# A decoder layer for prompt and samples: SyncE issues every transfer of the samples' key and value pages

## The chip, the cores and the metric

The kernel runs as one program on one core of a Trainium2 chip. The metric is the device time of one execution in microseconds (us), the median of several runs. All engines of the core take part: TensorE (PE) for matrix products and transposes, VectorE (DVE), ScalarE (ACT), GpSimd (POOL), and SyncE (SP), which computes nothing and only issues transfers. Each engine executes its own list of instructions in order and meets the others through semaphores. A transfer between device memory and the on-chip memory is issued by the instruction list of an engine; the bytes are then moved by the core's 16 DMA engines.

## What is computed

One layer of a hybrid decoder runs for a prompt of 512 tokens and for 8 sample sequences of 4 new tokens each. The part that the change touches is the attention of the samples. Each sample has 2048 past tokens, kept as 16 pages of 128 rows in a pool; a page table says which page of the pool holds which stretch of which sample. From the page rows the third and fourth parts, `k_sel` and `v_sel`, are the keys and values of the "selected blocks" branch:

```python
past = cache_kv[page_table].reshape(bsz, past_len, 4, NSA_KV, HEAD_DIM)
...
ks_t = full[:, :, 2].reshape(bsz, nb, BLK, NSA_KV, HEAD_DIM).transpose(0, 3, 1, 2, 4)
vs_t = full[:, :, 3].reshape(bsz, nb, BLK, NSA_KV, HEAD_DIM).transpose(0, 3, 1, 2, 4)
...
imp = jnp.where(allowed, imp, -FORCE_SCORE)
_, idx = lax.top_k(imp, k_sel)
...
s_s = jnp.einsum('bqgrd,bqgksd->bqgrks', qg, ks_g).reshape(bsz, tq, NSA_KV, NSA_REP, k_sel * BLK)
p_s = masked_softmax(s_s, s_mask)
o_s = jnp.einsum('bqgrn,bqgnd->bqgrd', p_s, vs_g)
s_w = jnp.einsum('bqgrd,bngd->bqgrn', qg, wk.astype(F32))
...
o = g[..., 0:1] * o_c + g[..., 1:2] * o_s + g[..., 2:3] * o_w
```

The kernel loads all 16 pages of every sample and applies the choice of blocks as a mask on the scores. A second branch attends to a window of 512 past tokens (`s_w`), a third to compressed blocks (`o_c`). State-space branch, cross-attention and the MLP stand before and after this stage and are not touched.

## The kernel before

**Stages in order.** Input projection and gate products; state-space branch; the samples' pages `k_cmp`, `v_cmp` are loaded (L664), relaid and compressed beside the prompt's attention (L1217 to L1299 on PE); then the samples' attention; then the memory keys, the branch outputs, cross-attention and the MLP. Everything on PE runs in the order in which it is written.

**The samples' attention** runs twice, for two groups (`gg` = 0 and 1) of four samples each. Its pages come in four batches per group, `kc` = 0 to 3: a batch is 4 pages of each of 4 samples, 16 transfers of 128 KB. The function `sel_pages(eng, gg, kc, known)` (L678 to L695) issues one batch on the engine that it is given:

- first it reads the 16 page numbers of the batch from the on-chip copy of the page table (L644: a register load, an operation on the register and a range check each), before any wait;
- then it waits: for group 1 until the four samples of group 0 are done (`sample_pv`, since both groups use one buffer `kv_pg`), for group 0 until the space is no longer used by the compression (`relaid` for `kc` 0, `cmp_done` for the others);
- then it issues the 16 transfers (L693), each counted on the semaphore `kv_in_kc`.

Before the change SyncE issues batches 0 and 1 and GpSimd batches 2 and 3 of each group, each on its own list. On SyncE other work stands between them: in group 0 the `weights(3)` after batch 0, three weight loads of 1 MB for the gate units 0 to 5, and in both groups, after batch 1, the window: for each of the 4 samples a transfer of keys (L809, semaphore `k_win_b`) and one of values (L810), 256 KB each. In group 1 `weights(1)`, one load of 1 MB, stands just ahead of the window.

**PE** takes the batches in the order `KC_ORDER` = (0, 2, 1, 3, 4), where 4 is the window. For each it waits for all 16 transfers, transposes the keys (L1329, 16 transposes) and, one batch behind, computes the scores (L1342); L1346 closes the group's scores. For `kc` = 4 it waits sample by sample:

```python
if kc == 4:
    pe.wait_ge(sem(f"k_win_{b}"), 16 * (gg + 1))
elif b == 0:
    pe.wait_ge(sem(f"kv_in_{kc}"), 16 * 16 * (gg + 1))
```

Then come a gate unit on PE (L999, while VectorE and ScalarE do the softmax), the transposes of the probabilities (L1368), and the product with the values (L1381), whose end is `sample_pv`. The gate units 2 to 4 (L999) run between the groups, and gate unit 0 (L999) ahead of group 0. The next group, and after the second group everything else, follows on PE in order.

Of the kernel before, what the change touches and what calls it, by code (L numbers as in the profile page):

```python
# [52 lines left out]
NG2 = 2  # L53
# [58 lines left out]
def hybrid_decoder_layer(nc, A, O):  # L112
# [7 lines left out]
    with ctx:  # L120
        sems = {}

        def sem(name):
            if name not in sems:
                sems[name] = ctx.enter_context(nc.semaphore(name))
            return sems[name]
# [12 lines left out]
        def place(cols, at=None):  # L139
            if at is None:  # L140
                at = top[0]
                top[0] += cols
            assert at + cols <= ACOLS and not at < ZS < at + cols, (at, cols)
            return upper[:, at - ZS:at - ZS + cols] if at >= ZS else arena[:, at:at + cols]
# [103 lines left out]
        CU = 4  # L248
# [55 lines left out]
        def keys_page(b, kc):  # L304

            return kv_pg[:, KV_AT[kc % 4], b, :, 0:P]

        qbd = place(256, R + 25920).rearrange("p (b c) -> p b c", b=DB)
# [141 lines left out]
        for m in range(4):  # L450
            for q in range(4):
                add(("down", m * 4 + q), KD, 256,
                    [(whole, cols(A["w_down"][0][q * 1024:(q + 1) * 1024, :], m * 256))])
        index = {name: i for i, (name, _) in enumerate(chunks)}
        arrived, _n = [], [0] * RING
        for i, (_, parts) in enumerate(chunks):
            _n[i % RING] += 16 * len(parts)
            arrived.append(_n[i % RING])
# [28 lines left out]
        late_at = {name: i for i, name in enumerate(late)}  # L487
        unsplit = ("in", "gate", "glu", "xk", "xv", "bs", "bn", "bs+bn")
        split_chunks = [i for i, (name, _) in enumerate(chunks) if name[0] not in unsplit]
        split_at = {chunks[i][0]: n for n, i in enumerate(split_chunks)}  # L490
        DN0 = split_at[("down", 0)]
# [112 lines left out]
        def step(name):  # L604

            return sem(step_of[name][0]), step_of[name][1]

        def signal(ins, name, n=1):
            if name in step_of:
                s, at = step_of[name]  # L610
                assert signalled.get(s, 0) == at - 1, (name, signalled)
                signalled[s] = at
                ins.then_inc(sem(s), 1)
            else:
                ins.then_inc(sem(name), n)
# [26 lines left out]
        def known_pages(eng, seqs, first, last):  # L642

            return {(q, p): eng.value_load(page_ids[0:1, q * PAGES + p:q * PAGES + p + 1], min_val=0, max_val=NPOOL - 1)  # L644
                    for q in seqs for p in range(first, last)}

        def raw_relaid(eng, j):

            for half in range(2):
                eng.wait_ge(sem(f"relaid_{half}"), j + 1)  # L650
# [27 lines left out]
        def sel_pages(eng, gg, kc, known):  # L678

            known.update({(gg * 4 + b, p): page for b in range(4)  # L680
                          for (_, p), page in known_pages(eng, (gg * 4 + b,), kc * 4, kc * 4 + 4).items()})
            if gg:
                eng.wait_ge(sem("sample_pv"), 4 * gg)
            elif kc == 0:
                raw_relaid(eng, 13)
            else:
                eng.wait_ge(sem("cmp_done"), 2 * CU - (kc == 2))
            for b in range(4):
                q = gg * 4 + b
                for i in range(4):  # L690
                    p = kc * 4 + i
                    page = known[q, p] if (q, p) in known else known_pages(eng, (q,), p, p + 1)[q, p]
                    eng.dma_start(kv_pg[:, KV_AT[kc], b, i:i + 1, :],  # L693
                                  A["cache_nsa_kv"][0][bass.ds(page, 1), :, 2:4].rearrange("n p z g d -> p n (z g d)"))\
                        .then_inc(sem(f"kv_in_{kc}"), 16)  # L695
# [5 lines left out]
        def _(sp):  # L701
# [3 lines left out]
            def weights(n=1):  # L705
                for _ in range(n):
                    i = nxt[0]
                    nxt[0] += 1
                    if i >= RING:
                        sp.wait_ge(*freed(i - RING))  # L710
                    for dst, src in chunks[i][1]:
                        sp.dma_start(dst, src).then_inc(w_sem[i % RING], 16)
# [50 lines left out]
            known = known_pages(sp, range(4), 0, SP_PAGES)  # L763
# [31 lines left out]
            win = A["cache_win_kv"][0]  # L795
            for gg in range(NG2):
                sel_pages(sp, gg, 0, known)
                if gg == 0:
                    raw_relaid(sp, 4 * CU - 1)
                    weights(3)  # L800
                sel_pages(sp, gg, 1, known)
                if gg == 0:
                    sp.wait_ge(*step("prompt_attn_done"))
                else:
                    weights(1)
                for b in range(4):
                    w = win[gg * 4 + b].rearrange("(n p) z g d -> z p n (g d)", p=P)
                    sp.wait_ge(sem("s_mm"), gg * 20 + b + 1)
                    sp.dma_start(keys_page(b, 4), w[0]).then_inc(sem(f"k_win_{b}"), 16)  # L809
                    sp.dma_start(v_win[:, b], w[1]).then_inc(sem("v_win_in"), 16)  # L810
# [65 lines left out]
        def _(pool):  # L876
# [39 lines left out]
            known = known_pages(pool, range(4), SP_PAGES, PAGES)  # L916
# [7 lines left out]
            for j in range(4 * CU):  # L924
# [8 lines left out]
                    zero_blocks(1, "w1b_zeroed")  # L933
                if j in (8, 9):
                    known.update(known_pages(pool, (j - 2,), SP_PAGES, PAGES))
            for gg in range(NG2):
                sel_pages(pool, gg, 2, known)
                if gg == 0:
                    pool.wait_ge(sem("cmp2_mm"), CU)
                    signal(pool.memset(qbd, 0.0), "qbd_zeroed")  # L940
                sel_pages(pool, gg, 3, known)

            def inverse_rms(n):

# [2127 lines left out]
```

## Time and profile before

| | us |
|---|---|
| median of 3 runs | 1246.42 (1246.36 to 1249.7) |
| time of the profiled execution | 1245.2 |
| its span | 1243.5 |
| PE busy | 1162.8 (94%) |
| DVE / ACT / POOL busy | 652.7 / 454.0 / 168.9 |

The span is what the trace covers; 1.7 us of the profiled execution's time lie around it. Instants are in us from the span's start. In the rows a number in front is the start, the next one the length. In square brackets stands how long an engine sat idle before a row and what ended that. SPq and POOLq are the instruction lists of SyncE and GpSimd; a transfer's row there is its issue, and its landing is told apart. Clock 1.00 in a row is TensorE at its upper level (2.4 GHz), and 0.50 would be the lower one (1.2 GHz).

### The profile page before, as it was taken

What the parts mean: (1) busy time and instruction counts of PE and PEld (TensorE: products, weight loads), DVE (VectorE), ACT (ScalarE), POOL (GpSimd) and SP (SyncE); (2) the same over time, 40 slices, a digit from 0 to 9 for tenths busy, and PEclk for the clock granted to TensorE, in tenths of its full rate; (3) what the DMA queues carried; (4) which work ended last, traced back from release to release, by engine and by line L of the source; (5) the groups of instructions that cost most, each with busy time, mean ns of one, the idle gap of its engine ahead of it and who ended that gap; (6) DMA issues with size and microseconds to landing.
All of it is one profiled execution on the core that took longest, in us unless ns stands there. A gap on an engine that the chain in (4) does not pass through costs nothing.

```text
span 1243.5 us, 21862 instructions
## 1 busy us (share of the span) xinstructions
PE 1162.8 (94%) x8426; PEld 1033.7 (83%) x8426; DVE 652.7 (52%) x1179; ACT 454.0 (37%) x726; POOL 168.9 (14%) x276
## 2 busy tenths in 40 slices
PE   6999988989989989889999997899999999999997
PEld 5888777667867757678897996789999999999997
DVE  3549857546656450511255556546443325666663
ACT  3100101045567451510133546446342325555551
POOL 0100012472531304100001002002000000001000
PEclk9999967989999999999999999899999998999998
DMA  6661512463563825655464643364353232223201
GB/s 191 145 211 38 175 46 94 128 170 97 148 160 93 268 81 188 220 190 150 138 206 132 225 136 112 121 242 136 102 170 102 71 100 69 72 99 102 69 1 72
DMA packets 166770, 163.88 MB, mean 132 GB/s; under 512 B 41526, under 2 KB 147859, under 8 KB 166459
## 3 DMA queue, kind: packets, MB, share of 16 engines
q1 hardware_dynamic: 157658, 134.84, 35.6%
q0 software_dynamic: 9008, 27.65, 7.0%
q8 instruction: 67, 1.10, 0.4%
q14 instruction: 37, 0.30, 0.1%
HBM read 154.08 MB, written 12.53 MB: 134 GB/s over the span
## 4 chain that ended last, share of the span: by engine, by line
PE 74%; SPq 9%; DVE 7%; issue 4%; ACT 3%; DMA 2%; POOL 0%; DVEq 0%; ACTq 0%
PE banks L1478 22%; PE banks L1733 14%; PE banks L999 14%; PE banks L1432 4%; SPq L664 3%; PE banks L1217 3%; SPq L644 2%; PE banks L1414 2%; PE banks L1005 1%; SPq L693 1%; PE banks L1120 1%; PE banks L1381 1%; DVE rounded L2803 1%; PE banks L1269 1%; PE banks L1329 1%
## 5 line engine op out<-in xcount | busy, mean ns | idle before, releaser
L1478 PE MATMUL banks<-rounded 128*128 128x288 f32 (+1 forms) x2304 | 298.1, 290 | 2.1 <-DVE rounded L2849 1.6
L1478 PEld LDWEIGHTS banks<-rounded 128*128 128x128 f32 x2304 | 292.7, 189 | 5.8 <-issue 2.9
L999 PE MATMUL banks<-arena 128*128 128x256 f32 x960 | 228.4, 399 | 3.2 <-issue 1.8
L999 PEld LDWEIGHTS banks<-arena 128*128 128x128 f32 x960 | 183.7, 193 | 40.4 <-issue 1.9
L1733 PE MATMUL banks<-rounded 128*128 128x272 f32 x1536 | 196.3, 291 | 3.8 <-DVE rounded L3031 3.8
L1733 PEld LDWEIGHTS banks<-rounded 128*128 128x128 f32 x1536 | 195.7, 191 | 4.4 <-issue 3.1
L2803 DVE TENSOR_TENSOR rounded<-arena,rounded 128x2048 fp32r<-128x2048 f32 x54 | 125.5, 2324 | 59.8 <-ACT rounded L1924 59.7
L3031 DVE TENSOR_TENSOR rounded<-arena,rounded 128x1088 fp32r<-128x1088 f32 x64 | 82.9, 1304 | 61.4 <-ACT rounded L2168 61.4
L1924 ACT ACTIVATE rounded<-arena 128x2048 fp32r<-128x2048 f32 x54 | 102.9, 1906 | 5.6 <-DMA arena<-in_w_out 5.6
L2168 ACT ACTIVATE rounded<-arena 128x1088 fp32r<-128x1088 f32 x64 | 71.1, 1114 | 82.2 <-PE banks L1733 81.0
L2964 DVE TENSOR_TENSOR arena<-arena 128x256 f32<-128x256 f32 (+1 forms) x64 | 28.1, 440 | 86.3 <-ACT arena L2009 86.3
L2009 ACT ACTIVATE arena<-banks 128x256 f32<-128x256 f32 (+1 forms) x64 | 25.4, 397 | 126.4 <-PE banks L1478 126.4
L1432 PE MATMUL banks<-arena 128*128 128x256 f32 (+1 forms) x256 | 60.5, 394 | 2.0 <-DVE arena L2795 2.0
L1432 PEld LDWEIGHTS banks<-arena 128*128 128x128 f32 x256 | 48.1, 190 | 12.5 <-DVE arena L2795 3.4
L970 POOL TENSOR_TENSOR upper<-upper 128x544 f32<-128x544 f32 x5 | 8.7, 1737 | 306.5 <-ACT upper L2179 306.3
L664 POOL DMA_DIRECT2D arena<-in_cache_nsa_kv x70 | 39.2, 563 | 65.2 <-issue 36.3
L693 POOL DMA_DIRECT2D upper<-in_cache_nsa_kv x64 | 34.5, 539 | 91.5 <-issue 52.0
L950 POOL TENSOR_SCALAR arena<-arena 128x1 f32<-128x1 f32 (+1 forms) x22 | 9.5, 432 | 258.4 <-ACT arena L1908 213.4
L1793 ACT ACTIVATE arena<-banks 128x256 f32<-128x256 f32 (+1 forms) x30 | 10.3, 393 | 93.6 <-PE banks L999 82.7
L2795 DVE TENSOR_TENSOR arena<-banks,arena 128x256 f32<-128x256 f32 (+1 forms) x32 | 14.1, 440 | 47.2 <-PE banks L1432 47.2
L1864 ACT ACTIVATE arena<-banks,arena 128x512 f32<-128x512 f32 (+3 forms) x64 | 33.1, 525 | 15.7 <-DVE arena L2613 15.6
L1858 ACT ACTIVATE arena<-banks 128x1024 f32<-128x1024 f32 (+3 forms) x32 | 22.5, 704 | 34.8 <-PE banks L1269 34.6
(432 smaller groups left out, 1462.9 us busy)
## 6 DMA issues: line engine op xcount, KB each, us to landing
arena<-in_w_up SPq DMA_DIRECT2D x22, 1024.0 KB, 5.5
arena<-in_w_down SPq DMA_DIRECT2D x16, 1024.0 KB, 5.1
arena<-in_w_in SPq DMA_DIRECT2D x13, 1024.0 KB, 6.9
upper<-in_cache_nsa_kv SPq DMA_DIRECT2D x64, 128.0 KB, 2.6
upper<-in_cache_nsa_kv POOLq DMA_DIRECT2D x64, 128.0 KB, 4.8
arena<-in_w_out SPq DMA_DIRECT2D x8, 1024.0 KB, 6.7
arena<-in_cache_mem_kv SPq DMA_DIRECT2D x16, 512.0 KB, 7.2
arena<-in_cache_nsa_kv SPq DMA_DIRECT2D x90, 64.0 KB, 2.3
```

What stands on the lines that cost most here:

```text
L664: eng.dma_start(rows[:, p:p + 1, :], A["cache_nsa_kv"][0][bass.ds(page, 1), :, v].rearrange("n p g d -> p n (g d)"))\
L693: eng.dma_start(kv_pg[:, KV_AT[kc], b, i:i + 1, :], A["cache_nsa_kv"][0][bass.ds(page, 1), :, 2:4].rearrange("n p z g d -> p n (z g d)"))\
L999: ins = mm(bank(b + h, (NA, NB)[h], rows=M), lhsT(k), rhs[:, k, toks], start=(k == 0), stop=(k == K - 1))
L1217: ins = mm(bank(6, n), w1[part][:, d % 32, :], relaid[part][:, d % 32, 0:n], start=(d == 0), stop=(d == HD - 1))
L1432: ins = mm(bank(b, N), c[:, k0 + k, c0:c0 + P], act[:, k, toks], start=(k == 0), stop=(k == 3))
L1478: ins = mm(bank(b, N), w[:, k], a[:, k, toks], start=(k == 0 and z == 0), stop=(k == K - 1 and z == 2))
L1733: ins = mm(bank(4 * (m % 2) + 2 * j + h, HALF), w[:, k, j * P:(j + 1) * P], h_split[:, t % 3, p, i, h * HALF:(h + 1) * HALF], start=(t % 1 ...
L1864: signal(fn(p_sb[:, i % 2, g, 0:n], bank(2 * (i % 2) + g, n), ACT.Exp, bias=nmx[:, at:at + 1], accum_out=rsum[:, at:at + 1]), "p_ready")
L1924: signal(fn(w_hi[:, n % 2], ring[:, i % RING, :], ACT.Copy), "w_hi")
L2168: signal(fn(h_split[:, t % 3, 0], h_tiles(t), ACT.Copy), "h_hi")
L2803: signal(tt(w_lo[:, n % 2], ring[:, split_chunks[n] % RING, :], w_hi[:, n % 2].bitcast(F32), ALU.subtract), "w_lo")
L3031: signal(tt(h_split[:, t % 3, 1], h_tiles(t), h_split[:, t % 3, 0].bitcast(F32), ALU.subtract), "h_lo")
```

## The change

Batches 2 and 3 of both groups move from GpSimd's list to SyncE's, in the order in which PE takes the batches: 0, 2, 1, 3. GpSimd keeps the `memset` of `qbd` and its wait.

```diff
             for gg in range(NG2):
                 sel_pages(sp, gg, 0, known)
+                sel_pages(sp, gg, 2, known)
                 if gg == 0:
                     raw_relaid(sp, 4 * CU - 1)
                     weights(3)
                 sel_pages(sp, gg, 1, known)
+                sel_pages(sp, gg, 3, known)
                 if gg == 0:
                     sp.wait_ge(*step("prompt_attn_done"))
                 else:
...
-            for gg in range(NG2):
-                sel_pages(pool, gg, 2, known)
-                if gg == 0:
-                    pool.wait_ge(sem("cmp2_mm"), CU)
-                    signal(pool.memset(qbd, 0.0), "qbd_zeroed")
-                sel_pages(pool, gg, 3, known)
+            pool.wait_ge(sem("cmp2_mm"), CU)
+            signal(pool.memset(qbd, 0.0), "qbd_zeroed")
```

The number of transfers and their bytes stay. The page numbers of each moved batch are now read by SyncE, 64 reads more on its list. Line numbers behind the first edit grow by two (L809 becomes L811).

**SyncE, group 0.** L644 are the reads of page numbers (16 in a block), L693 the page transfers (16 in a batch), L712 weights, L809 and L810 the window. Before:

```order
L693 ISA [waits relaid_1,relaid_0]
L693 DMA upper<-in_cache_nsa_kv 128x256
...
L712 DMA arena<-in_w_in 128x8x256 [waits lin_done,relaid_1,relaid_0]
L712 DMA arena<-in_w_in 128x8x256 [waits lin_done] x2
L644 TENSOR_LOAD page_ids
L644 ISA x2
...
L693 ISA [waits cmp_done]
L693 DMA upper<-in_cache_nsa_kv 128x256
...
L809 DMA upper<-in_cache_win_kv 128x4x128 [waits s_mm,vector_steps_done]
L810 DMA arena<-in_cache_win_kv 128x4x128
```

The same stretch of SyncE after the change, where L811 and L812 are the window:

```order
L693 ISA [waits relaid_1,relaid_0]
...
L644 TENSOR_LOAD page_ids
...
L693 ISA [waits cmp_done]
...
L712 DMA arena<-in_w_in 128x8x256 [waits lin_done,relaid_1,relaid_0]
L712 DMA arena<-in_w_in 128x8x256 [waits lin_done] x2
...
L693 ISA [waits cmp_done]
...
L693 ISA [waits cmp_done]
...
L811 DMA upper<-in_cache_win_kv 128x4x128 [waits s_mm,vector_steps_done]
L812 DMA arena<-in_cache_win_kv 128x4x128
```

A block of reads and a batch now stand between batch 0 and the weights, and another block and batch between batch 1 and the window.

**GpSimd, group 0.** Before, batches 2 and 3 stood around the `memset` (L940):

```order
L644 TENSOR_LOAD page_ids
L644 ISA x2
...
L693 ISA [waits cmp_done]
L693 DMA upper<-in_cache_nsa_kv 128x256
...
L940 MEMSET upper 128x256 [waits cmp2_mm]
...
L693 ISA [waits cmp_done]
...
L693 ISA [waits sample_pv]
```

Of this only the `memset` and its wait stay on GpSimd. In group 1 both moved batches go ahead of the weight load and the window on SyncE, as in group 0; the order on PE is unchanged.

## Rows read from the trace of the kernel before

**Rows 1.** The page: busy time of each engine, and the chain by engine.

```profile
PE 1162.8 (94%) x8426; PEld 1033.7 (83%) x8426; DVE 652.7 (52%) x1179; ACT 454.0 (37%) x726; POOL 168.9 (14%) x276
PE 74%; SPq 9%; DVE 7%; issue 4%; ACT 3%; DMA 2%; POOL 0%; DVEq 0%; ACTq 0%
```

**Rows 2.** Timeline of PE, group 0: gate unit 0, transposes, scores, gate unit 1.

```profile
425.51 7.60 PE L999 MATMUL banks<-arena 128*128 128x256 f32 x32
...
437.67 1.95 PE L1329 MATMUL banks<-arena,upper 128*128 128x128 f32 x16
...
443.43 1.97 PE L1329 MATMUL banks<-arena,upper 128*128 128x128 f32 x16
...
449.69 0.66 PE L1329 MATMUL banks<-arena,upper 128*128 128x128 f32 x4 [0.89 <-DMA upper<-in_cache_win_kv]
450.28 3.61 PE L1342 MATMUL banks<-upper 128*32 128x512 f32 x16
...
454.90 7.57 PE L999 MATMUL banks<-arena 128*128 128x256 f32 x32 [0.89 <-issue]
```

**Rows 3.** Timeline of PE, group 1, from the gate units between the groups on.

```profile
473.30 22.17 PE L999 MATMUL banks<-arena 128*128 128x256 f32 x96
...
498.72 1.94 PE L1329 MATMUL banks<-arena,upper 128*128 128x128 f32 x16
...
505.09 3.53 PE L1329 MATMUL banks<-arena,upper 128*128 128x128 f32 x16 [3.44 <-DMA upper<-in_cache_nsa_kv]
...
512.44 2.19 PE L1329 MATMUL banks<-arena,upper 128*128 128x128 f32 x16
514.56 1.93 PE L1342 MATMUL banks<-upper 128*32 128x512 f32 x16
516.30 0.31 PE L1346 MATMUL banks<-arena,upper 128*32 128x32 f32 x16
```

**Rows 4.** Timeline of SyncE's list, both groups (start, length, issues).

```profile
391.01 8.69 SPq L693 DMA_DIRECT2D upper<-in_cache_nsa_kv  x16
399.80 7.25 SPq L712 DMA_DIRECT2D arena<-in_w_in  x3
416.36 9.88 SPq L693 DMA_DIRECT2D upper<-in_cache_nsa_kv  x16
440.67 0.39 SPq L809 DMA_DIRECT2D upper<-in_cache_win_kv  x1
...
472.94 26.71 SPq L693 DMA_DIRECT2D upper<-in_cache_nsa_kv  x32
499.69 0.50 SPq L712 DMA_DIRECT2D arena<-in_w_in  x1
501.67 0.39 SPq L809 DMA_DIRECT2D upper<-in_cache_win_kv  x1
```

**Rows 5.** Timeline of GpSimd, the batches of both groups.

```profile
398.68 9.45 POOL L693 DMA_DIRECT2D upper<-in_cache_nsa_kv  x16 [32.08 <-issue]
416.55 0.32 POOL L940 MEMSET upper<- 128x256 f32 x1 [8.42 <-PE banks L1235]
473.41 9.44 POOL L693 DMA_DIRECT2D upper<-in_cache_nsa_kv  x16 [36.34 <-PE banks L1381]
```

**Rows 6.** Landing of transfers: the weights at 399.8 to 400.9, then batch 0.

```profile
DMA to landing us min/median/max: 11.5/15.1/17.5
DMA to landing us min/median/max: 2.0/2.2/3.3
```

**Rows 7.** Busy time, clock, DMA share and GB/s in stretches of the span.

```profile
400.00:417.00 17.00, 17.00 (x151) 13.15 (x150) 9.36 (x27) 9.63 (x23) 7.71 (x15) 1.00 0.98 324
497.00:517.00 20.00, 16.16 (x138) 11.35 (x136) 9.71 (x19) 11.36 (x23) 3.96 (x8) 0.91 1.07 349
182.00:204.00 22.00, 11.81 (x164) 10.59 (x162) 13.67 (x44) 4.27 (x4) 4.26 (x8) 0.69 0.46 139
```

**Rows 8.** Timeline of PE: 32 products of a gate unit's size early in the span.

```profile
172.75 9.81 PE L999 MATMUL banks<-arena 128*128 128x256 f32 x32
```

## The prediction, made before the changed kernel ran

> **What bounds the kernel now.** I read the page first. PE is busy 94% of the span and carries 74% of the chain that ended last; SyncE's list is the second largest part of that chain, with 9%, and POOL has none of it [rows 1]. So what SyncE does late can already hold PE up, and what GpSimd does is off the path. Then I read the timelines of PE, SyncE and GpSimd side by side over the samples' attention, since the order of PE is fixed and only the arrival of pages can move it.
>
> Before group 0, PE has gate unit 0 at 425.51 and then takes batches 0, 2, 1, 3 one after the other, the fourth at 443.43; it waits 0.89 us for the last window keys, resumes at 449.69, and starts gate unit 1 at 454.90 [rows 2]. In group 1 the gate units 2 to 4 cover 473.30 to 495.47 (start plus length). Then PE waits 3.44 us for the pages of batch 1, resumes at 505.09 and ends the scores at 516.61 (516.30 + 0.31) [rows 3]. The pages are hardly late now, because two lists issue them at once: SyncE needs 8.69 us for a batch of 16 and GpSimd 9.45 us or 9.44 us, over the same time [rows 4, 5].
>
> **The price of a batch on SyncE.** Issuing takes 8.7 us. The row of 32 issues in group 1 lasts 26.71 us [rows 4]. Two batches of 8.69 explain 17.38 of it; the other 9.3 us are the 16 reads of page numbers ahead of the second batch. The gap in group 0 between the end of the weights at 407.05 and batch 1 at 416.36 is 9.3 us too [rows 4]. So one more batch costs 9.3 + 8.7 = 18.0 us of SyncE's time. Four such batches are moved, and none of their reads can run earlier, since the list is in order. What hid them before was GpSimd's own list, and that cover goes.
>
> **Group 0, step by step on SyncE** (the instants of before are kept until something moves).
> - Batch 0 ends at 391.01 + 8.69 = 399.7 [rows 4]. Reads 9.3 and batch 2, 8.7, end at 417.7. GpSimd issued batch 2 from 398.68 on [rows 5], so the wait for `cmp_done` is over long before.
> - The three weight loads follow. They took 7.25 us before, because the third issue had to wait [rows 4], in a stretch where the DMA engines were full (share 0.98, 324 GB/s) [rows 7] and GpSimd's batch was in the same engines. Without a full engine it would be about 1.5 us (three issues of 0.50, as the one at 499.69 [rows 4]). After the change nothing competes, but 3 MB still queue: some 1.2 MB must drain before the third is accepted. This is my estimate from half of 324 GB/s over the 7.25 us; at the full rate the same bytes take about 4 us. I take 5.0 us and 0.1 of gap, ends 1.5 and 7.25. That gives 422.8.
> - Reads 9.3, batch 1 8.7, reads 9.3, batch 3 8.7: 458.8. Batch 1 took 9.88 before [rows 4], with the weights still landing; I keep 1.2 us for the upper end.
> - The window starts there instead of at 440.67. Before, PE resumed on the last window keys at 449.69, 9.0 us later [rows 2, 4]; now 467.8. From there to gate unit 1 it was 454.0 - 449.7 = 4.3 us without the idle 0.89 [rows 2]; the scores end at 472.1 instead of 454.0. **Group 0: +18.1 us**, ends +14.6 and +21.5.
>
> Two waits appear inside this and cost nothing extra. Behind SyncE's batch 2 stand the weights of gate unit 0, which land some 7 to 11.5 us after issue (the lower end my estimate for an empty queue, from 1 MB at 324 GB/s and the 3.3 us landing of a page transfer; the upper end measured [rows 6, 7]), at 425 to 429 against a need at 425.51. A delay of up to 4 us there is covered, since PE will sit waiting for batches 1 and 3 anyway: batch 3 lands near 461 (2.2 us after its issue [rows 6]) against a start at 443.43 before. And GpSimd's `memset` waits only for a PE product and ran at 416.55 [rows 5]; it can only come earlier.
>
> **Group 1**, counted from the end of group 0, which has moved as a whole. SyncE reads batch 0's numbers before the wait, in idle time, as before. From 472.94 it issues batch 0, reads, issues batch 2 until 499.65, exactly the 26.71 us that batches 0 and 1 took [rows 4]. Batches 1 and 3 with their reads add 36.0: 535.7. Then the weight load and the window. In group 0 the window alone took 9.0 us from first issue to PE's resuming. In group 1 it took about 14.3 us from 499.69 to the last transposes (near 514.0, the last quarter of the row at 512.44) [rows 3, 4], of which 1.5 us (500.19 to 501.67) were a wait for PE that is over by then; and then the engines were overfull (share 1.07, 349 GB/s) [rows 7]. One MB more than group 0's window at 324 GB/s is 3.2 us, so 9.0 + 3.2 = 12.2; against 14.3 - 1.5 = 12.8 I take 12.5, ends 9.0 and 14.3. PE resumes at 548.2, and 4.3 us later, as in group 0, the scores end at 552.5, against 516.6: **+35.9 us**. With group 1's own tail of 2.6 us (514.0 to 516.6) it would be 1.7 less; ends +30.7 and +37.7.
>
> **The clock.** PE will idle for some 15 us in group 0 and 30 us in group 1. The granted clock fell to 0.91 in 497 to 517 around an idle of 3.44 us, and to 0.69, a mix of both levels, in 182 to 204, where PE was busy 11.81 of 22 us [rows 7]. Just after such a sparse stretch work runs at the lower level: transposes took 3.53 us for 16, instead of 1.97 [rows 2, 3]. Part of this is in the 4.3 us. A gate unit that was partly caught cost 9.81 us instead of 7.57 [rows 2, 8], 2.2 more. I add 1 us per group, 2.0, ends 0 and 5.
>
> **Nothing gives it back.** After group 1 everything on PE stands behind `sample_pv`, and the memory loads too. What the change removes is GpSimd's work, off the path, and the 3.44 and 0.89 us of waiting are replaced by longer waits. Sum: 18.1 + 35.9 + 2.0 = 56.0 us. The profiled execution took 1245.2, so it would take 1301.2; the median of before lies 1.2 above that execution, so 1302. The ends add to +45 and +64: 1291 to 1311.
>
> **The rule against this.** The rows show that the issue of one 128 KB transfer by SyncE takes 8.69 / 16 = 0.54 us, and with the read of its page number 1.13 us [rows 4], while its bytes at 349 GB/s [rows 7] need 0.38 us: here the list, not the DMA engines, is what limits. The Trainium skill, page "DMA: Bandwidth & Descriptors", section "Issuing engines are not separate DMA queues", says that transfers started by SyncE, ScalarE or GpSimd run on the same 16 engines, and that issuing from several only saves the sequencer's time, "which is usually small relative to the DMA itself". By its first half the change would cost nothing; its "usually" fails on these rows by a factor of three. As a rival it stands below, worked out in rows.
>
> **The rivals.**
> - *Bytes set the pace, no change.* If only the bytes counted, group 1's 8 MB of pages, 1 MB of weights and 2 MB of window at 349 GB/s take 33 us from 472.94 on, to 506, ahead of PE's need at 512.44: about 1246. For it speaks that the engines were full in two stretches [rows 7]; against it that SyncE's 32 issues alone lasted 26.71 us. By the skill's sentence this is the expected case. Chance 0.04.
> - *Faster.* The right order ends the wait for batch 1 (3.44), the clock dip behind it (3.53 - 1.97 = 1.6) and the wait for the window (0.89): -5.9 us, about 1240. This holds only if four batches are issued while gate units 2 to 4 run, 22.17 us, so below 5.5 us a batch; measured is 8.7 without the reads. Chance 0.04.
> - *The reads are hidden*, because registers keep the numbers or the reads overlap the issues. Then the four extra blocks of 9.3 us drop out: 56.0 - 37.2 = 18.8, about 1265. Against it: the reads stand in SyncE's list between the batches, and the existing block shows up in full in the 26.71. Chance 0.05.
> - *Dearer.* Gate unit 0 waits for its weights and the lower clock lasts through the gate units behind each group (two more units at 2.2 us, and 3 to 5 us for slower landings): above 1311. Chance 0.07.
>
> **Chances.** The forecast, 1291 to 1311, has 0.80, and the range is its own. Below it lie the three cheaper cases, 0.13 together. A measurement of this kernel tells a change from none at about 0.3%, 4 us. Faster 0.04, same 0.04, slower 0.92.
>
> **What would show each step right.** On SyncE, three blocks of about 9.3 us between four batches of 8.7 in each group; batch 3 of group 1 issued some 62.7 us after the first (26.71 + 36.0). On PE, long waits for pages ahead of the third and fourth batch, then for the window, at L1329 in both groups; gate unit 1 starting some 18 us later, the last score of group 1 some 54 to 56 us later; all stages from there on as long as before. Wrong would be the forecast if SyncE's blocks shrink, if the weight loads stall much longer than 7 us, or if PE's later stages change length.

## The result: slower by 3.3 to 3.4%

| | us |
|---|---|
| changed kernel, median of 4 runs | 1288.73 (1285.95 to 1293.24) |
| changed kernel once more, median of 5 runs | 1288.71 (1286.71 to 1291.5) |
| kernel before, median of 17 runs beside the second measurement | 1248.75 (1242.15 to 1252.71) |
| ratio, first and second measurement | 1.0342 (1.0313 to 1.037), 1.0333 (1.0304 to 1.0363) |

The brackets hold the fastest and the slowest run, for a ratio its 95% interval. The change costs 40 to 42 us. I had forecast 56 us and 1291 to 1311: the direction and the place are right, the size is not, and the time lies 2.3 us under my range.

The page of the changed kernel, engines and chain, answers to [rows 1]:

```profile
span 1284.3 us, 21862 instructions
...
PE 1161.9 (90%) x8426; PEld 1031.0 (80%) x8426; DVE 651.1 (51%) x1179; ACT 455.0 (35%) x726; POOL 134.3 (10%) x212
...
PE 67%; SPq 15%; DVE 7%; issue 6%; ACT 2%; DMA 2%; POOL 0%; DVEq 0%; ACTq 0%
...
L1327 PE MATMUL banks<-arena,upper 128*128 128x128 f32 x160 | 25.4, 321 | 46.7 <-DMA upper<-in_cache_nsa_kv 45.0
```

PE does the same work (1162.8 us before), SyncE's part of the chain went from 9% to 15%, and one line, the transposes of the page keys (L1327, before L1329: behind the edit of GpSimd's list the line numbers fall by two), has 46.7 us of PE's idle time ahead of it, 45.0 of them ended by page transfers. GpSimd gave up 34.6 us of work that had been on nobody's path.

The timeline of SyncE's list, against [rows 4]. The row of 32 issues is two batches with one block of reads between, the row of 64 four batches with three blocks:

```profile
387.53 26.33 SPq L693 DMA_DIRECT2D upper<-in_cache_nsa_kv  x32
413.97 4.90 SPq L712 DMA_DIRECT2D arena<-in_w_in  x3
427.80 25.85 SPq L693 DMA_DIRECT2D upper<-in_cache_nsa_kv  x32
453.77 0.39 SPq L811 DMA_DIRECT2D upper<-in_cache_win_kv  x1
...
484.09 60.95 SPq L693 DMA_DIRECT2D upper<-in_cache_nsa_kv  x64
545.08 0.43 SPq L712 DMA_DIRECT2D arena<-in_w_in  x1
```

The timeline of PE over both groups, against [rows 2, 3]; the brackets hold the idle time ahead of a row:

```profile
422.04 7.60 PE L997 MATMUL banks<-arena 128*128 128x256 f32 x32
...
438.57 1.97 PE L1327 MATMUL banks<-arena,upper 128*128 128x128 f32 x16 [1.45 <-DMA upper<-in_cache_nsa_kv]
...
455.97 3.67 PE L1327 MATMUL banks<-arena,upper 128*128 128x128 f32 x16 [14.44 <-DMA upper<-in_cache_nsa_kv]
...
463.13 1.92 PE L1340 MATMUL banks<-upper 128*32 128x512 f32 x16
...
466.05 7.57 PE L997 MATMUL banks<-arena 128*128 128x256 f32 x32 [0.88 <-issue]
...
511.91 1.97 PE L1327 MATMUL banks<-arena,upper 128*128 128x128 f32 x16 [1.88 <-DMA upper<-in_cache_nsa_kv]
...
529.32 3.67 PE L1327 MATMUL banks<-arena,upper 128*128 128x128 f32 x16 [14.45 <-DMA upper<-in_cache_nsa_kv]
...
547.62 3.67 PE L1327 MATMUL banks<-arena,upper 128*128 128x128 f32 x16 [12.76 <-DMA upper<-in_cache_nsa_kv]
...
556.72 1.92 PE L1340 MATMUL banks<-upper 128*32 128x512 f32 x16
...
559.65 7.57 PE L997 MATMUL banks<-arena 128*128 128x256 f32 x32 [0.88 <-issue]
```

The long waits are 12.8 to 14.5 us. In group 0 there is one, for batch 3; batch 1 is only 1.45 us late, since it had been early before. In group 1 there are two, for batches 1 and 3; batch 2 is late too, by 1.88 us. Meanwhile the DMA engines have time to spare. These are stretches of the changed kernel (columns as in [rows 7]) in which batches are being issued, the last with PE mostly waiting:

```profile
400.00:417.00 17.00, 16.21 (x150) 12.34 (x146) 10.53 (x32) 10.99 (x25) 0.32 (x1) 1.00 0.49 153
...
490.00:517.00 27.00, 22.22 (x125) 17.79 (x123) 7.53 (x15) 7.73 (x17) 0.00 (x0) 1.00 0.37 113
517.00:545.00 28.00, 5.54 (x24) 3.48 (x24) 0.69 (x1) 2.39 (x4) 0.00 (x0) 0.58 0.47 141
```

A share of 0.37 to 0.49, where the kernel before had 0.98 and 1.07 in its busiest stretches [rows 7].

### The profile page after: what moved, and what is told of

It reads as the page before. It is cut to its first block, busy times and chain, and to the rows that moved or that the text cites. A ratio compares the mean times of both kernels' runs of the same rounds, so it can differ in the third digit from the quotient of the medians.

```text
span 1284.3 us, 21862 instructions
## 1 busy us (share of the span) xinstructions
PE 1161.9 (90%) x8426; PEld 1031.0 (80%) x8426; DVE 651.1 (51%) x1179; ACT 455.0 (35%) x726; POOL 134.3 (10%) x212
## 4 chain that ended last, share of the span: by engine, by line
PE 67%; SPq 15%; DVE 7%; issue 6%; ACT 2%; DMA 2%; POOL 0%; DVEq 0%; ACTq 0%
PE banks L1476 21%; PE banks L1731 14%; PE banks L997 13%; SPq L644 5%; SPq L693 4%; PE banks L1430 4%; SPq L664 3%; PE banks L1412 2%; PE banks L1215 1%; PE banks L1003 1%; PE banks L1379 1%; DVE rounded L2801 1%; DMA upper<-in_cache_win_kv 1%; PE banks L1118 1%; SPq L771 1%
## 5 line engine op out<-in xcount | busy, mean ns | idle before, releaser
L1327 PE MATMUL banks<-arena,upper 128*128 128x128 f32 x160 | 25.4, 321 | 46.7 <-DMA upper<-in_cache_nsa_kv 45.0
L1327 PEld LDWEIGHTS banks<-arena,upper 128*128 128x128 f32 x160 | 22.0, 166 | 54.5 <-DMA upper<-in_cache_nsa_kv 49.5
L1885 ACT ACTIVATE upper<-banks 128x512 f32<-128x512 f32 x40 | 21.8, 604 | 57.2 <-PE banks L1327 57.1
```

The source lines that it names most:

```text
L1327: ins = pe.transpose(bank(KT_BANKS[b], P, i * P), keys_page(b, kc)[:, i, :], ident)
```

## Experiments

A difference in us is the measured ratio times the time of the kernel before; that of the two medians differs from it by up to 2 us. Two theories stood at the start. **A**: SyncE's list sets the pace, by its issues and by its reads of page numbers, which stand in order with them. **B**: the reads lie beside other work, and the issues or the bytes are what costs. A group's cost in a trace comes from three starts on PE, gate unit 0, gate unit 1 and the gate unit behind group 1: in the kernel before 425.51, 454.90 [rows 2] and 517.49, in the changed kernel 422.04, 466.05 and 559.65. They moved by -3.5, +11.1 and +42.2 us, so group 0 costs 11.1 + 3.5 = 14.6 us and group 1 42.2 - 11.1 = 31.0. The row of before that [rows 3] do not have:

```profile
517.49 7.57 PE L999 MATMUL banks<-arena 128*128 128x256 f32 x32 [0.88 <-issue]
```

**The reads taken away.** The three later batches use batch 0's page numbers.

```diff
-            known.update({(gg * 4 + b, p): page for b in range(4)
...
+            if kc == 0:
...
-                    page = known[q, p] if (q, p) in known else known_pages(eng, (q,), p, p + 1)[q, p]
+                    page = known[q, i]
```

> The changed kernel, but the page numbers of batches 2, 1 and 3 are not read: all four batches of a group fetch the pages of batch 0 (so the output is computed from the wrong past rows; the transfers keep their number, size and order). Theory A, SyncE's list is the limit and a read block costs it 8.9 us: six blocks leave the list between batches. Group 0: 387.5 + 2 x 8.7 + 4.9 + 2 x 8.7 = 427, ahead of PE, so no loss. Group 1: four batches end 34.8 us after the group before, the window 11 us later and the scores 2.6 us after that, 48.4 us against 43.7 before: +5 us. In all 1252, within 4 us. Theory B, the reads lie beside other work and the 128 issues are what costs: within 5 us of the changed kernel, 1284 to 1293.

Measured: 1253.37 us, ratio 1.005 (1.0028 to 1.0072), +6 us against the kernel before. Nearly the whole loss is gone, as A wants. (This run also fetches the same pages four times over; a run with the right pages, below, gets most of the loss back too.) The list in this trace:

```profile
390.84 16.24 SPq L693 DMA_DIRECT2D upper<-in_cache_nsa_kv  x32
...
475.15 32.81 SPq L693 DMA_DIRECT2D upper<-in_cache_nsa_kv  x64
```

Four batches take 32.81 us, 8.2 each. With the reads they took 60.95, so a block of 16 reads costs (60.95 - 32.81) / 3 = 9.4 us of the list.

**The reads added, nothing else moved.**

```diff
                 sel_pages(sp, gg, 0, known)
+                known_pages(sp, range(gg * 4, gg * 4 + 4), 8, 12)
...
                 sel_pages(sp, gg, 1, known)
+                known_pages(sp, range(gg * 4, gg * 4 + 4), 12, 16)
```

> The kernel before, where SyncE in addition reads the 16 page numbers of batch 2 behind batch 0, and those of batch 3 behind batch 1, and does nothing with them; GpSimd issues batches 2 and 3 as before. Theory A: group 0 +1 to +3 us (window from 442 on instead of 440.7), group 1: batch 1 issued until 508.4 (499.7 before), window from 517 on, scores end at 531 instead of 516.6, +14 us. In all +16 us, 1264, within 4 us. Theory B: reads cost nothing, within 4 us of the kernel before. A third, that SyncE's reads and GpSimd's get in each other's way: a read takes clearly more than the 0.55 us of before and the loss is above 20 us.

Measured: 1262.25 us, ratio 1.0123 (1.0098 to 1.0148), +15 us. The reads alone, with GpSimd issuing its batches as ever, cost more than a third of the loss. The third theory in the expectation falls too: SyncE's register loads took 0.26 to 0.28 us as before, also from 484.8 to 493.0, where GpSimd read its own numbers. SyncE's 32 issues of group 1 now span two blocks instead of one, 35.53 us instead of 26.71, and the window follows a third block later:

```profile
475.48 35.53 SPq L693 DMA_DIRECT2D upper<-in_cache_nsa_kv  x32
519.87 0.39 SPq L712 DMA_DIRECT2D arena<-in_w_in  x1
```

**One group at a time.** The other group's batches 2 and 3 stay on GpSimd.

```diff
+                if gg == 0:
+                    sel_pages(sp, gg, 2, known)
...
+            sel_pages(pool, 1, 2, known)
+            sel_pages(pool, 1, 3, known)
```

> Only group 0 has batches 2 and 3 on SyncE (order 0, 2, 1, 3); group 1 is issued as before, batches 2 and 3 by GpSimd. To keep GpSimd's and SyncE's counts apart, SyncE's two moved batches count on semaphores that are done with their first use. If the loss is the sum of two stages: group 0's part as in the trace of the changed kernel, +14.7 us, group 1's part zero: 1263, within 4 us. If the groups depend on each other (group 0's delay gives SyncE or the clock something back in group 1): below +9 us or above +20.

> Only group 1 has batches 2 and 3 on SyncE; group 0 is issued as before. Semaphores as in the run with group 0 alone. If the loss is the sum of two stages: +31 to +33 us, 1280, within 4 us, and with the run of group 0 alone it adds up to the change's +41 to +46. If group 1 costs what I forecast for it, 36 to 37 us: 1284 or more.

Measured: group 0 alone 1256.83 us, ratio 1.0071 (1.0044 to 1.0098), +9 us; its trace has +13.0 us in group 0. Group 1 alone 1277.97 us, 1.0255 (1.0224 to 1.0286), +32 us; its trace has +31.0 in group 1. The two add up to +41, as the whole change, so the groups cost what they cost separately. Group 1 costs 31 to 32 us, not the 36 to 37 that I forecast. For group 0 the expectation of 1263, within 4, was missed: +9 us lies on the edge that I had set for groups that depend on each other. What speaks against that is the sum. Why the timed runs show 9 us (5.5 to 12.2 by the interval) where three traces have 13.0 to 14.6 is not shown.

**Half the bytes.** The transfers fetch the keys and leave out the values.

```diff
-                    eng.dma_start(kv_pg[:, KV_AT[kc], b, i:i + 1, :],
-                                  A["cache_nsa_kv"][0][bass.ds(page, 1), :, 2:4]...
+                    eng.dma_start(kv_pg[:, KV_AT[kc], b, i:i + 1, 0:P],
+                                  A["cache_nsa_kv"][0][bass.ds(page, 1), :, 2]...
```

> The changed kernel, but each page transfer fetches the keys only, 64 KB instead of 128 KB (the values are left out, so the output is not the layer's). Issues, reads and order stay. If SyncE's list sets the pace, a batch still takes 8.4 to 8.7 us and the time stays within 4 us of the changed kernel (1285 to 1293); the third weight load may be accepted up to 2 us sooner. If the bytes or the landing set it, the two groups' waits shrink with the bytes: below 1275.

Measured: 1287.91 us, ratio 1.0312 (1.0283 to 1.0341); the changed kernel has 1288.7. Group 1's four batches and the weights in group 0:

```profile
417.66 2.71 SPq L712 DMA_DIRECT2D arena<-in_w_in  x3
...
487.09 60.98 SPq L693 DMA_DIRECT2D upper<-in_cache_nsa_kv  x64
```

60.98 us against 60.95 with all the bytes: the bytes have no part in the pace of the page batches. Only the weights behind them were taken sooner, 2.71 us instead of 4.90. This also settles the rule that I had set against the trace. The Trainium skill ("DMA: Bandwidth & Descriptors", "Issuing engines are not separate DMA queues") calls the sequencer's time "usually small relative to the DMA itself". The traces disagree for these transfers of 128 KB: 0.51 us of issue and 0.59 us of reading the address, against 0.38 us for the bytes at the 349 GB/s of [rows 7].

**Batch 2 alone moved, in both groups.**

```diff
                 sel_pages(sp, gg, 0, known)
+                sel_pages(sp, gg, 2, known)
...
-                sel_pages(pool, gg, 2, known)
```

> Only batch 2 of both groups moves to SyncE; GpSimd keeps batch 3. By the list's arithmetic: group 0, batch 1 lands as late as in the changed kernel (PE waits 1.5 us), the window starts near 440 as before: +2 us. Group 1: batch 1 is issued until 43.4 us after the group before (516.3), the window is complete 11.1 us later, the scores end at 530 instead of 516.6: +13.5 us. Together +15.5 us, 1263, within 4. If instead each moved batch costs the same, half of the change's loss: +21 us, 1268 or more.

Measured: 1260.14 us, ratio 1.008 (1.0052 to 1.0108), +10 us, less than my +15.5, though within 4 us of the 1263, and clearly less than half of the loss. Its trace has the waits for batch 1 at the places forecast: 3.38 us in group 0, where I expected 1.5, and 14.69 us in group 1. A moved batch does not have a fixed price; it depends on how early the batches behind it had been. Why the timed runs give less than the 16 us that the trace of this stage shows against the one trace of before stays open; the spread of single executions, below, is larger than the gap.

**Numbers read ahead.** In the changed kernel SyncE reads 48 numbers, those of batches 0, 2 and 1, before it waits for a group:

```diff
+            if kc in (0, 3):
...
+            if kc == 0:
+                known.update({(gg * 4 + b, p): page for b in range(4)
+                              for (_, p), page in known_pages(eng, (gg * 4 + b,), 4, 12).items()})
```

> The changed kernel, but SyncE reads the numbers of batches 0, 2 and 1 (48 of them) before it waits for the group, and only those of batch 3 between batches; all pages are the right ones. One visible read block a group instead of three. Group 0: all four batches issued by 387.5 + 8.7 + 8.7 + 4.9 + 8.7 + 8.9 + 8.7 = 436, window on time, 0 to +1 us. Group 1: 32.8 + 8.9 = 41.7 us for the batches, window 11.1, tail 2.6: 528.3 instead of 516.6, +12 us. In all +12 us, 1259, within 4. If reads ahead of the wait are not free (they delay batch 0), +18 or more.

Measured: 1265.87 us, ratio 1.0135 (1.0102 to 1.0167), +17 us: 23 us of the 40 come back, and my +12 is missed. Reading ahead was not free here. 48 reads are longer than SyncE's idle time ahead of group 0. Batch 0 starts at 396.91, where it was 391.01 in the kernel before, with gate unit 0 at nearly the same place (426.01 and 425.51):

```profile
396.91 18.15 SPq L697 DMA_DIRECT2D upper<-in_cache_nsa_kv  x32
415.17 2.79 SPq L716 DMA_DIRECT2D arena<-in_w_in  x3
418.16 30.01 SPq L697 DMA_DIRECT2D upper<-in_cache_nsa_kv  x32
448.28 0.39 SPq L815 DMA_DIRECT2D upper<-in_cache_win_kv  x1
...
480.29 43.95 SPq L697 DMA_DIRECT2D upper<-in_cache_nsa_kv  x64
```

There is a second cost. The batches 1 and 3 of group 0, with one block of reads between them, take 30.01 us here and 25.85 in the changed kernel. No block of reads stands between the weights and batch 1 any more; the engines are full (share 1.02 from 415 to 432), and single issues of pages take up to 2.64 us instead of 0.33. In group 1 the list needs 43.95 us for four batches and a block, where 32.81 + 9.4 = 42.2 would do.

In the kernel before, both lists read the numbers of their two batches, 32, ahead of the wait:

```diff
-            known.update({(gg * 4 + b, p): page for b in range(4)
-                          for (_, p), page in known_pages(eng, (gg * 4 + b,), kc * 4, kc * 4 + 4).items()})
+            if kc in (0, 2):
+                known.update({(gg * 4 + b, p): page for b in range(4)
+                              for (_, p), page in known_pages(eng, (gg * 4 + b,), kc * 4, kc * 4 + 8).items()})
```

> The kernel before, but SyncE and GpSimd each read the numbers of both their batches (32) before they wait for the group, in time in which they idle. Group 1's batch 1 is then issued until 490.4 instead of 499.7; even with full DMA engines (8 MB at 349 GB/s: 24 us, until 497) it is there before PE asks at 501.7. That ends the wait of 3.44 us and the clock dip behind it (1.6 us), but the window can start only at 500.6, when PE has used batch 0, and PE may wait 1 to 3 us for it: -2 to -5 us, 1242 to 1245. If page transfers on two queues at once block each other more than in the trace, no gain.

Measured: 1242.72 us, ratio 0.9967 (0.9942 to 0.9992). Once more, in five rounds:

> The kernel before with all page numbers of a group read ahead of its wait on both lists, once more for a narrower interval: 3 to 6 us below the kernel before. If the first result (-4 us, interval from -7 to -1) was chance, within 2 us.

Measured: 1243.0 us, ratio 0.996 (0.9938 to 0.9982), 5 us faster than the kernel before. The waits of PE for page transfers are gone from its trace, and the window's are left, 3.2 us in three (first trace, 430 to 520):

```profile
PE banks L1330 <- DMA upper<-in_cache_win_kv: 3.2, 3, 1.4
```

**Window keys first**, on top of this:

```diff
                     sp.dma_start(keys_page(b, 4), w[0]).then_inc(sem(f"k_win_{b}"), 16)
+                for b in range(4):
+                    w = win[gg * 4 + b].rearrange("(n p) z g d -> z p n (g d)", p=P)
                     sp.dma_start(v_win[:, b], w[1]).then_inc(sem("v_win_in"), 16)
```

> As the kernel with numbers read ahead, and in each group the four transfers of window keys are issued ahead of the four of window values instead of in turns. In the trace of that kernel PE still waits 3.2 us for window keys (three waits). The last keys are then issued 3 x 0.54 = 1.6 us sooner and with 0.75 MB less ahead of them (2.3 us at 324 GB/s): the waits go, -2 to -3 us against the kernel with numbers read ahead. If the keys were late because each is issued only when PE has used the slot, less than 1 us.

Measured: 1237.79 us (1235.47 to 1239.81), ratio 0.9912 (0.9884 to 0.9939): 11 us faster than the kernel before, 5 us faster than with the numbers read ahead alone, more than the 2 to 3 expected. The timeline of SyncE has the four key transfers in 2.04 us, and in PE's timeline no transfer is waited for:

```profile
502.84 2.04 SPq L810 DMA_DIRECT2D upper<-in_cache_win_kv  x4
504.92 3.29 SPq L813 DMA_DIRECT2D arena<-in_cache_win_kv  x4
```

This version beats both kernels. Against the kernel with numbers read ahead the gain is less sure: the two intervals, 0.9884 to 0.9939 and 0.9938 to 0.9982, just touch. Why it exceeds the waits removed was not followed further.

**The changed kernel again**, for the part of the difference that lies outside the stage.

> The changed kernel once more, unaltered, for its time in more runs and a second trace. In the first trace the stages ahead of the samples' attention were 3.5 us faster than in the trace of the kernel before and those behind it 2.7 us faster, though nothing in them differs. If that is the placing of short low-clock stretches by chance, the second trace does not repeat the full -6 us, the samples' attention alone costs 45 to 48 us again, and the ratio lies at 1.034 to 1.038. If the change itself speeds those stages up, the -6 us come back.

Measured: ratio 1.0333 (1.0304 to 1.0363), a little under the 1.034 expected. I count the stage from gate unit 0 to the 64 products of a gate unit that start at 584.34 in the kernel before, at 628.17 in the changed one and at 630.25 in its second trace. In the second trace the stages ahead are as long as before (+0.4 us, not -3.5), the stage costs 45.6 us (47.3 in the first), and the stages behind it are 2.5 us shorter (3.0 in the first). The mean granted clock (the third column from the end, ahead of the DMA share) early in the span, in the kernel before, the changed one, and the changed one again:

```profile
140.00:215.00 75.00, 64.02 (x405) 53.97 (x404) 48.91 (x166) 6.59 (x12) 13.16 (x18) 0.77 0.32 99
```

```profile
140.00:215.00 75.00, 63.74 (x419) 53.23 (x418) 52.15 (x166) 6.59 (x12) 15.11 (x22) 0.82 0.34 102
```

```profile
140.00:215.00 75.00, 63.44 (x405) 53.58 (x404) 48.78 (x173) 6.59 (x12) 12.91 (x18) 0.77 0.33 99
```

0.77, 0.82, 0.77: the clock there differs between executions of one kernel, and the -3.5 us ahead of the stage did not come back.

## Why the prediction was right, and where it failed

**Right**: what bounds the stage. SyncE's list took over, every batch with its reads costs it 18 us (measured 17.6 = 8.2 + 9.4), group 0 loses on batch 3 and the window, group 1 on batches 1 and 3 and the window. The three weight loads took 4.90 us, my estimate was 5.0; the second trace has 3.34. Gate unit 0 was not held up, GpSimd gave nothing back, and the stages behind keep their length to 3 us. The share of the clock in these 3 us is not shown. The three cheaper rivals fell: the bytes by the run with half of them, the freed wait by the waits of 12.8 to 14.5 us, and the hidden reads by the first two experiments. The dearer one did not come either.

**Failed**: the sizes after the last batch, nearly all on the same side.

| step (group 0; group 1) | forecast | trace |
|---|---|---|
| SyncE, first batch to window | 67.8; 62.7 | 66.2; 61.0 |
| window's first issue (in group 1 the weights') to PE resuming on the last keys | 9.0; 12.5 | 8.8; 11.1 |
| from there to the end of the scores | 4.3; 4.3 | 2.6; 2.6 |
| cost of the group | 18.1; 35.9 | 14.6; 31.0 |
| clock, beyond these | 2.0 together | 1.7 (second trace 0) |

The 1.7 us are in one row of the product with the values, which took 3.70 us in the kernel before:

```profile
572.82 5.37 PE L1379 MATMUL banks<-upper,arena 128*32 128x128 f32 x128
```

The steps of the stage sum to 8.7 us of the miss in the first trace (56.0 against 47.3) and to 10.4 in the second. The one that failed most is "From there to gate unit 1 it was 454.0 - 449.7 = 4.3 us", used for both groups: it measured 2.6 in both. The 4.3 us hold a stretch of low clock: the 16 products of L1342 took 3.61 us [rows 2], and in group 1 1.93 [rows 3]. That stretch did not belong to the group's end. After the change the slow work is where PE resumes from its long wait (the transposes at 455.97, 529.32 and 547.62 take 3.67 us instead of 1.97), where the next wait for a transfer hides most of it; by the last keys the clock is back, and L1340 takes 1.92 us. Both traces of the changed kernel have this in both groups, but it is not certain in every execution: in the run with half the bytes the 16 products at the end of group 1 took 2.99 us. I let one dip count in the tail (from the last keys to the end of the scores) of both groups, 3.4 us of the miss, and "I add 1 us per group" added 2.0 for the clock again, of which the first trace has 1.7, elsewhere, and the second nothing. The bounds helped too little, since the tail of 2.6 us, which I had from [rows 3], was allowed for group 1 only. But no single step explains the miss: with that tail allowed in group 0 too, my lower end would have been 1.7 us lower, still above what was measured.

The second term is the batch: 8.7 us was measured with GpSimd's transfers in the same engines. Alone, a batch takes 8.2 us (60.95 us less three blocks of 9.4, by four; 25.85 less one, by two), and 8.5 in the first row of group 0. From the first batch to the window this makes 3.3 us over both groups, as much as the tail. The third is the window in group 1: its 12.8 us were from the overfull engines of before; I took 12.5, and 11.1 came.

**The frame.** I set the median 1.2 us above the profiled execution. Over 17 runs it is 1248.75, 3.5 above it. That alone would have put the forecast higher, further off. Against it, the stages outside were 6.5 us shorter in the changed kernel's first trace and 2 in the second. Traces give the stage's cost as 47.3 and 45.6 us; the timed runs give 40 to 42. So the steps above explain 9 to 10 of the 14 to 16 us between my 56 and the measured cost, and the rest stays open. Part of it may be the one trace of before, whose execution was 3.5 us faster than the median of its kernel: if these 3.5 us lie in the stage, which is not shown, every cost read against that trace is too large by them. I take the timed runs for the size and the traces for the place.

## What to carry to other kernels

Price a transfer by all that its issuer must do for it in order, the read of its address too: here 0.59 us for the read and 0.51 us for the issue against 0.38 us for the bytes. Two lists that issue at once are worth having when that sum is larger than the bytes' time, and address reads belong into the issuer's idle time ahead of a wait, but no more of them than fit there: 32 ahead on each list gained 5 us, 48 on one list started the first batch 6 us late. Before a duration is carried over to another place, look whether a dip of the clock lies in it; otherwise the dip is counted where it may not be.

## What the runs showed of the hardware

The granted clock differs between executions at the same place in the program (0.77 and 0.82 over the same 75 us), and between the same two traces of one kernel the start of the stage lies 3.8 us apart (422.04 and 425.87). The kernel before spreads from 1242.15 to 1252.71 us over 17 runs, so a single pair of traces cannot size a change of 5 us. A short low-clock stretch came with PE's first work after each long wait: in the three places of the first trace where PE had waited over 12 us, 16 transposes took 3.67 us each time, in those of the second 3.46, 3.67 and 3.68; after a wait of 1.45 us they took 1.97. In the kernel before it was 3.53 us after a wait of 3.44 [rows 3]. Such stretches are not bound to a wait: the product with the values took 5.37 us instead of 3.70 with no wait over 0.8 us just before it.

An issue can take far longer than its usual half microsecond. The third of three 1 MB loads in a row took 6.18 us in the kernel before, 3.83 in the changed kernel and 1.62 in its second trace; a lone one took 0.50 [rows 4]. What decides between these is not shown: the DMA share over the three loads was 0.93, 0.93 and 0.77.
